# Spacing the splits of cross-attention weights evenly over a feed-forward block, and resharing the taps of a convolution

## The reference, cut to what matters

```
# first block, its end
h2 = rmsnorm(x, g_ffn)
ff = silu(h2 @ w_ffn_gate) * (h2 @ w_ffn_up)        # 1024 -> 2816
x  = x + ff @ w_ffn_down                            # 2816 -> 1024
# second block, layer 0
h = rmsnorm(x, norm_mix_g)
u = h @ w_pw1 + b_pw1;  a, gate = split(u);  u = a * sigmoid(gate)
u = conv_general_dilated(u, w_dw, width 31, causal, one filter a channel) + b_dw
u = silu(layernorm(u));  x = x + u @ w_pw2 + b_pw2
...
# keys and values of a memory of 256 rows, in both layers (nothing here depends on x)
k = rmsnorm(mem, g_l) @ w_k_l;   v = rmsnorm(mem, g_l) @ w_v_l
```

## Time and profile before

| what | value |
|---|---|
| median, range of three runs | 2281.22 us, 2280.41 to 2285.22 |
| the profiled execution, whole | 2279.9 us |
| its span from first to last instruction | 2277.7 us |
| TensorE busy | 2219.8 us (97%) |
| VectorE, ScalarE, GpSimd busy | 1340.5, 975.5, 406.4 us |
| mean granted TensorE clock | 0.996 |

### The profile page before, as it was taken

How to read it: one execution, slowest core, us unless ns; L and a number is a source line. 1 busy time by engine, 2 the same in 40 slices (tenths; PEclk the granted TensorE clock), 3 DMA queues, 4 the chain that set the end, 5 groups by cost and what they waited for, 6 DMA issues and landing times.

```text
span 2277.7 us, 31273 instructions
## 1 busy us (share of the span) xinstructions
PE 2219.8 (97%) x10680; PEld 1800.2 (79%) x10680; DVE 1340.5 (59%) x1904; ACT 975.5 (43%) x1486; POOL 406.4 (18%) x338
## 2 busy tenths in 40 slices
PE   8999999998998999989999999999999999999998
PEld 6787788877776878868888888887777888888887
DVE  5567756554555679975465445485655646454455
ACT  6775654432333367763332222245454333222222
POOL 2232102101010247834040000040000304000003
PEclk9999999999999999999999999999999999999999
DMA  4222223467676455642123333332222212333332
GB/s 148 65 66 63 76 80 96 145 177 230 179 204 200 148 173 187 215 156 74 56 82 95 93 101 102 92 87 77 66 56 60 88 57 83 102 93 98 96 96 89
DMA packets 413080, 253.36 MB, mean 111 GB/s; under 512 B 14832, under 2 KB 394224, under 8 KB 412976
## 3 DMA queue, kind: packets, MB, share of 16 engines
q1 hardware_dynamic: 412080, 249.68, 36.7%
q0 software_dynamic: 896, 2.33, 0.3%
HBM read 232.56 MB, written 18.87 MB: 110 GB/s over the span
## 4 chain that ended last, share of the span: by engine, by line
PE 78%; DMA 7%; DVE 5%; issue 3%; ACT 2%; SPq 1%; POOLq 1%; DVEq 1%; POOL 0%; ACTq 0%
PE bank L1951 22%; PE bank L1953 21%; PE bank L1952 21%; DMA m_raw<-in_w_ffn_up 3%; PE bank L1931 2%; DVE m_w_lo L1260 2%; DMA m_raw<-in_w_ffn_down 2%; PE bank L2424 1%; POOLq L670 1%; PE bank L2401 1%; DMA mem_low<-m_mem_raw_lo 1%; PE bank L2339 1%; PE bank L2329 1%; PE bank L2104 1%; PE bank L2530 1%
## 5 line engine op out<-in xcount | busy, mean ns | idle before, releaser
L695 ACT ACTIVATE m_w_hi<-m_raw 128x1024 fp32r<-128x1024 f32 x332 | 351.4, 1059 | 844.1 <-PE bank L1953 693.8
L1951 PE MATMUL bank<-m_h_hi,m_w_hi 128*128 128x512 f32 x1504 | 608.2, 404 | 17.1 <-DVE m_w_lo L1260 15.8
L1953 PE MATMUL bank<-m_h_hi,m_w_lo 128*128 128x512 f32 x1504 | 587.0, 390 | 0.0
L1952 PE MATMUL bank<-m_h_lo,m_w_hi 128*128 128x512 f32 x1504 | 586.4, 390 | 0.0
L1260 DVE TENSOR_TENSOR m_w_lo<-m_raw,m_w_hi 128x1024 fp32r<-128x1024 f32 x332 | 444.7, 1339 | 133.3 <-ACT m_w_hi L695 127.4
L1951 PEld LDWEIGHTS bank<-m_h_hi,m_w_hi 128*128 128x128 f32 x1504 | 282.6, 188 | 94.0 <-DVE m_w_lo L1260 19.9
L1953 PEld LDWEIGHTS bank<-m_h_hi,m_w_lo 128*128 128x128 f32 x1504 | 282.3, 188 | 60.1
L1952 PEld LDWEIGHTS bank<-m_h_lo,m_w_hi 128*128 128x128 f32 x1504 | 282.9, 188 | 54.8 <-issue 2.2
L1951 PE MATMUL bank<-m_f_hi,m_w_hi 128*128 128x512 f32 x688 | 269.5, 392 | 7.4 <-DVE m_w_lo L1260 7.3
L1953 PE MATMUL bank<-m_f_hi,m_w_lo 128*128 128x512 f32 x688 | 267.9, 389 | 0.0
L1952 PE MATMUL bank<-m_f_lo,m_w_hi 128*128 128x512 f32 x688 | 267.8, 389 | 0.0
(11 more groups left out here) (399 smaller groups left out, 3222.6 us busy)
## 6 DMA issues: line engine op xcount, KB each, us to landing
m_raw<-in_ff_w SPq DMA_DIRECT2D x256, 256.0 KB, 3.0
mem_low<-m_mem_raw_lo SPq DMA_DIRECT2D x32, 512.0 KB, 3.3
m_mem_w_low<-mem_low SPq DMA_DIRECT2D x32, 512.0 KB, 7.3
m_raw<-in_conv_pw_w SPq DMA_DIRECT2D x48, 256.0 KB, 3.1
m_raw<-in_w_in SPq DMA_DIRECT2D x47, 256.0 KB, 3.3
m_raw<-in_w_ffn_gate SPq DMA_DIRECT2D x44, 256.0 KB, 5.2
m_raw<-in_w_ffn_up SPq DMA_DIRECT2D x44, 256.0 KB, 5.1
m_raw<-in_w_ffn_down SPq DMA_DIRECT2D x40, 256.0 KB, 5.1
```

The costliest lines, as they stand in the source:

```text
L695: act.activation(WH[:, v % 2], RAW[:, v % 2], ACT.Copy).then_inc(s.w_hi, 1)
L1951: pe.matmul(o, high[:, r, k, :], hi, start=start, stop=False)
L1952: pe.matmul(o, high[:, r, k, :], lo, start=False, stop=False)
L1953: last = pe.matmul(o, low[:, r, k, :], hi, start=False, stop=stop)
```

## The change

`MEM_SPLIT_AT` names every second unit from 4 to 66. Before, it named 4 to 14 in steps of 2, every unit from 16 to 23, 24 to 38 in steps of 2, every unit from 40 to 47, and 48 and 50. The stores stand one place later on SyncE's list. So the last splits and stores reach into the loads of the convolution stage, and `conv_loads` passes them out.

In the convolution, each of the first seven tiles gives 12 taps to ScalarE and GpSimd (13 before) and 19 to VectorE (18 before). The last tile gives 8 to ScalarE and GpSimd (10 before), 6 to TensorE (3 before) and 17 to VectorE (18 before). On ScalarE the high part of memory piece 0 stands ahead of the norm's root, that of piece 25 ahead of the last tile's sigmoid, and the last tile's first four products ahead of piece 26.

```diff
-SUM_TAPS = 13
-SUM_TAPS_LAST = 10
+SUM_TAPS = 12
+SUM_TAPS_LAST = 8
-MEM_SPLIT_AT = (4, 6, 8, 10, 12, 14) + tuple(range(16, 24)) + tuple(range(24, 40, 2)) + tuple(range(40, 48)) + (48, 50)
+MEM_SPLIT_AT = range(4, 4 + 2 * MEM_UNITS, 2)
-PE_TAPS_LAST = 3
+PE_TAPS_LAST = 6
@@ SyncE
-                split_at.setdefault(ffn + n + 5, []).append(lambda i=i: split_out(i))
+                split_at.setdefault(ffn + n + 6, []).append(lambda i=i: split_out(i))
@@ mem_load
+                stored(i)
@@ last group
-                    assert not split_at
-                    for i in range(MEM_UNITS - 4, MEM_UNITS):
-                        stored(i)
@@ conv_loads
                 for half in range(2):
+                    splits()
@@ after conv_loads(0), conv_loads(1)
+            while split_at:
+                for f in split_at.pop(min(split_at)):
+                    f()
+            for i in range(MEM_UNITS - 4, MEM_UNITS):
+                stored(i)
@@ VectorE conv_steps
-                cut = [0, 9, DVE_TAPS]
+                cut = [0, 10, DVE_TAPS]
@@ ScalarE conv_steps
                 if m == 0:
+                    mem_high(first)
                     norm()
...
-                mem_high(first)
+                if m > 0:
+                    mem_high(first)
...
+                if m == KD - 1:
+                    mem_high(last)
                 act.wait_ge(s.cv_g, m + 1)
...
             last = SUM_TAPS_LAST, PE_TAPS_LAST
-            mem_high(25)
+            products(KD - 1, 0, 4, *last)
             mem_high(26)
-            products(KD - 1, 0, 4, *last)
             mem_out(24)
-            products(KD - 1, 4, 7, *last)
+            products(KD - 1, 4, 6, *last)
             mem_high(27)
-            products(KD - 1, 7, SUM_TAPS_LAST, *last)
+            products(KD - 1, 6, SUM_TAPS_LAST, *last)
```

## The result

The kernel after takes 2249.03 us (median of four runs, 2247.36 to 2250.44), the kernel before in the same series 2283.03 us (four runs, 2280.41 to 2285.22). The ratio is 0.9851, with a 95% interval of 0.9834 to 0.9868: faster by 34 us. The forecast was 2254 us with a gain of 27.6.

What follows compares the result with a forecast made beforehand. TensorE, busy 2219.8 of 2277.7 us, was taken as the bound. The terms -24.5 + 3.5 - 2.8 + 0.8 - 4.6 = -27.6 us took 2279.9 to 2252.3, given as 2254 on the median's side; range 2246 to 2267.

Steps and rivals of the forecast that it cites:

- The feed-forward's waits: Feed-forward stretches with splits: stores behind the up load remove all 22.5 us of waits, plus restarts, -24.5 us.
- Rival C: Feed-forward: the spacing does nothing, 32 splits still cost 24 us, only tail and start pay, 2278 us; chance 0.04.
- D: Feed-forward: the up unit's load lands too late at each of 32 splits, slower, 2297 us; chance 0.03.
- the term for restarts: Feed-forward: each restart after a wait costs TensorE 0.11 us, times 22 is 2.4 us.
- The 0.4 us kept for a stray wait: Feed-forward: of 24.9 us of waits and restarts, 0.4 us was held back for a stray wait.
- The added splits: 722 to 803 us, last group: eight more splits cost +3.5 us, 1.5 at unit 60's load and 2.0 on VectorE.
- Rival B: Last eight units: VectorE becomes the bound by its exclusion with GpSimd, +6 instead of +2, 2263 us; chance 0.07.
- The convolution's start: TensorE starts 1.2 us sooner with piece 0's high part early, 1.6 us of clock return, -2.8 us (0 to -4).
- The middle: Convolution tiles: VectorE bounds tiles 2 to 4, one tap more costs 2.0 us, less 1.2 us elsewhere, +0.8 us.
- tiles 2 to 4 no shorter than before: Sign expected in the profile after: convolution tiles 2 to 4 don't get shorter; no size given.
- The tail: Last tile to squares' sum: products run while a landing is awaited, two sums fewer, -4.6 us (-2 to -7).
- rival A: Feed-forward: half of the waits remain, -12 in place of -24.5, 2266 us; chance 0.08.

Runs made afterwards that it cites:

- Experiment 1: The kernel after with each store back at its old place, ahead of the up load, even spacing kept: 2276.54 us.
- experiment 2: The kernel after with the old table of splits, stores behind the up load except in the rows of eight: 2253.44 us.
- experiment 10: The kernel of experiment 3 with VectorE's first seven low parts of the normed memory set between the down units: 2244.6 us.
- experiment 3: The kernel after with all 32 splits done before the last group's down units: 2242.38 us.
- experiment 6: The kernel after with 13 products a tile on ScalarE, 12 additions on GpSimd and one VectorE tap fewer, last tile as changed: 2250.67 us.
- experiment 7: The kernel after with the last tile's old division (10 products on ScalarE, 3 taps on TensorE, 18 on VectorE), new order kept: 2247.82 us.
- experiments 4: The kernel of experiment 3 with the six DMAs for memory pieces 0 to 2 spread over the last group's down units: 2240.66 us.
- experiment 9: The kernel after with the high parts of memory pieces 29 to 31 moved later on ScalarE, among and behind the squares: 2246.23 us.

## Why the prediction was right, and where it was not

**The feed-forward's waits: 24.5 us forecast, 29.1 found (331.28 to 302.14).** The mechanism is the one forecast. In after the up load is issued at 559.73, the store at 560.87 behind it; ScalarE's high part then waits for TensorE, no longer for a landing as in the earlier trace rows.

```profile
559.73 0.92 SPq L399 DMA_DIRECT2D m_raw<-in_w_ffn_up  x2
560.87 0.34 SPq L489 DMA_DIRECT2D mem_low<-m_mem_raw_lo  x1
```

```profile
566.58 1.06 ACT L699 ACTIVATE m_w_hi<-m_raw 128x1024 fp32r<-128x1024 f32 x1 [2.91 <-PE bank L1960]
```

Experiment 1 shows that most of it is the store's place (22.4 us), and experiment 2 that the evenly spaced waits vanish with it. Rival C describes the kernel of experiment 1, not this one; D is out. The size was off by 4.6 us, nearly all of it in the term for restarts, which I set to 0.11 us a wait. TensorE in after, at the boundary of two units:

```profile
571.53 0.39 PE L1960 MATMUL bank<-m_h_hi,m_w_lo 128*128 128x512 f32 x1
571.76 0.39 PE L1958 MATMUL bank<-m_h_hi,m_w_hi 128*128 128x512 f32 x1
```

Without a wait the next matmul starts 0.16 us before the end of the one before it. The profile counts idle time from that end, so a wait costs the idle time, the 0.16 us of lost overlap, the 0.11 us by which the second matmul comes later, and 0.03 us spread over the next four. That is 0.30 us for each of 22 waits, 6.7 us instead of 2.4: 22.5 + 6.7 = 29.1. The 0.4 us kept for a stray wait was not needed, since none came. The 6.7 us are counted as busy time. The clock at the convolution's start takes 1.4 of them back, the last group's new waits 0.9 and the stretch ahead of unit 4 0.4; in the tail three more taps (2.6 us) and the full clock that came back there nearly cancel (0.2). Together with hundredths elsewhere that leaves the 3.8 us above.

**The added splits: +3.5 forecast, +4.2 found.** From unit 59 to the first down unit's start after loses 1.71 us (1.5 forecast). Across the kernels with the same program up to there this wait was 1.04 to 1.98 us. SyncE is held up issuing behind the store, ScalarE waits, TensorE waits:

```profile
729.38 0.71 SPq L489 DMA_DIRECT2D mem_low<-m_mem_raw_lo  x1
730.13 4.04 SPq L399 DMA_DIRECT2D m_raw<-in_w_ffn_down  x2
```

```profile
740.37 1.06 ACT L699 ACTIVATE m_w_hi<-m_raw 128x1024 fp32r<-128x1024 f32 x1 [7.97 <-DMA m_raw<-in_w_ffn_down]
```

```profile
742.74 0.50 PE L1958 MATMUL bank<-m_f_hi,m_w_hi 128*128 128x512 f32 x1 [1.70 <-DVE m_w_lo L1267]
```

The rest, 2.5 us, is VectorE (2.0 forecast). A low part of a memory piece takes 2.31 us there:

```profile
764.12 2.31 DVE L1603 TENSOR_TENSOR m_mem_raw_lo<-m_mem_raw,m_mem_raw_hi 128x1024 fp32r<-128x1024 f32 x1
```

```profile
763.79 1.55 POOL L595 TENSOR_TENSOR m_sumsq<-m_sumsq,m_sq 128x512 f32<-128x512 f32 x1
```

GpSimd's sum started first and ends at 765.34; 1.22 us from there is 766.56, and the row ends at 766.43. The Trainium skill's "SBUF — State Buffer", section "SBUF: two separate sides", says that whichever of the two starts first keeps the other out for its whole length; it says so of a VectorE instruction with two SBUF inputs and a GpSimd one that reads SBUF. Here and in experiment 10 (0.4 us of work, 1.5 us long) the trace agrees to 0.2 us. TensorE lost 0.87 and 0.79 us, two restarts and some tenths to it; the rule's upper end of 6 us was not reached. Rival B's direction was thus real and its price too high; experiment 3 shows that the whole term was avoidable.

**The convolution's start: -2.8 forecast, +0.8 found. This step failed.** The forecast put TensorE's start at VectorE's lows plus one split of 1.2 to 1.5 us. The mechanism held: high part early, VectorE late.

```profile
782.78 2.30 DVE L1603 TENSOR_TENSOR m_mem_raw_lo<-m_mem_raw,m_mem_raw_hi 128x1024 fp32r<-128x1024 f32 x1
...
785.04 3.21 DVE L1609 SCALAR_TENSOR_TENSOR m_mn_lo<-m_mem_cols,m_vec,m_mn_hi 128x256 fp32r<-128x256 f32 x8
```

But the last split took 2.30 us beside GpSimd, so the wait only fell from 3.79 to 3.13 us. Net, the arrival is 0.55 us sooner instead of 1.2. And the clock, from which I took 1.6 us back, did not come back; it cost 1.4 us more. The ten microseconds behind the first memory product in the kernel before:

```profile
813.50:823.50 10.00, 10.00 (x49) 9.04 (x50) 1.22 (x1) 3.08 (x4) 0.00 (x0) 0.84 0.49 159
```

The same ten microseconds behind the same matmul in after:

```profile
788.30:798.30 10.00, 9.99 (x43) 9.12 (x44) 1.79 (x2) 2.81 (x4) 0.00 (x0) 0.69 0.48 145
```

and in experiment 6, then in experiment 7, both with the same 3.13 us wait:

```profile
787.40:797.40 10.00, 9.96 (x48) 8.90 (x49) 1.82 (x2) 2.83 (x4) 0.00 (x0) 0.83 0.52 158
```

```profile
787.00:797.00 10.00, 10.00 (x55) 8.79 (x56) 2.66 (x4) 4.07 (x6) 0.00 (x0) 1.00 0.49 159
```

One wait, three outcomes: 27.9, 26.6 and 25.1 us for the stage, with the same instructions up to there in all three. I treated the granted clock as a result of the wait's length and so as something an edit could return; at 3.1 us something decides that these runs don't show. The clock did stay at its full level in the kernels that waited 1.3 to 1.9 us there (experiments 2 to 4, all 25.11 us); experiment 1 waited 2.49 us there and lost it (26.64 us).

**The middle: +0.8 forecast, -1.4 found.** The step that failed is that VectorE bounds tiles 2 to 4. It was read from its busy share. What ends TensorE's waits there is ScalarE's high part, and ScalarE is late by its products and by waiting for GpSimd's additions (12.8 us before, 1.2 after). One product and one addition fewer a tile are worth 2.1 us in the middle and 1.3 in the tail (experiment 6); the forecast gave the shorter chain 1.2 us and took 2.0 off for VectorE. It had named a shorter GpSimd chain only as its lower bound. With thirteen products the middle takes 0.7 us more than in the kernel before, so something else in the change costs about that; the runs don't say what, and it is within the range of this stage. The sign "tiles 2 to 4 no shorter than before" did not come true: the three tiles from the third on take 62.95 us and took 63.52.

**The tail: -4.6 forecast, -4.8 found** (46.10 to 41.34). One wait of 1.95 us ended by ScalarE, none for the last tile, as forecast:

```profile
972.21 1.12 PE L2391 MATMUL bank<-m_ln_sq,m_con 128*128 128x512 f32 x2 [1.95 <-ACT m_ln_sq L1100]
```

```profile
950.66 2.57 ACT L1038 ACTIVATE m_tap_product<-m_padded,m_vec 128x512 f32<-128x512 f32 x4 [1.09 <-DVE m_padded L1684]
...
968.69 2.95 ACT L1014 ACTIVATE m_mem_w_high<-m_mem_w 128x1024 fp32r<-128x1024 f32 x3 [1.61 <-DMA m_mem_w_low<-mem_low]
971.55 0.61 ACT L1100 ACTIVATE m_ln_sq<-m_conv 128x512 f32<-128x512 f32 x1
```

The four products run at 950.66, ahead of the landings; the three high parts and then the first square are the floor that the forecast named as last, and experiment 9 took it away. Within the term the way was not as told: TensorE idles 4.9 us less, of which 2.5 us is ScalarE's copy of the key piece's product, awaited 3.08 us before and 0.58 us after, which the forecast did not list. The three taps cost 2.6 us, and 2.4 us came back from the clock, which was at its slow level (1.2 GHz) behind the 4.39 us wait ahead of the mean and is at full speed in after (1.00). That the total was met to 0.2 us is partly luck.

**The sum.** From unit 4 on: -29.1 + 4.2 + 0.8 - 1.4 - 4.8 = -30.2 us, from unrounded terms; a difference of 0.3 us ahead of it and 0.1 behind make it the 29.8 of the two spans. The errors are -4.6 (feed-forward, restarts above all), +0.7 (added splits), +3.6 (start), -2.2 (middle) and -0.2 (tail). They leave -2.6 us of a sum of absolute errors of over 11: that the total came so near is luck in the start and the middle. The remaining 4 us to the medians' 34 lie in how the kernel before ran in the first series: its profiled execution was 3.1 us under its median of 2283.0, and after's was 0.7 us above its own.

**The forecast's own arithmetic.** Its range of 2248 to 2261 leaves out the -12 that it names as the first term's bound (that is rival A). With the other bounds in squares the upper end comes out as 2261, the lower as 2249.6, and the measured 2249.03 lies just below that, inside the 2246 to 2267 that was given. The 0.88 us a split at which D "decides slower" is where D meets the kernel before; for 4.6 us more it takes 1.02.

## What to carry to other kernels

A load that starts late can be the fault of what stands ahead of it in its own queue: put what waits for a late result (here a store) behind what can already go, before changing how often it occurs. Price a wait of TensorE as its idle time plus what the restart loses (0.30 us here), and don't count on getting a slow clock back when an edit shortens the wait by only some tenths. Ask not which engine is busiest but which one ends the wait, and what on its list stands ahead of the awaited step without being needed yet.

## What was not expected of the hardware

A wait of 3.13 us at the same place of the same program was followed by a granted clock over 10 us of 1.00, 0.83 or 0.69, from one kernel to the next; 3.08 us in the tail of the kernel before was followed by full speed (0.36 us for the first matmul of 128x256, where a slow one takes 0.55), 3.49 us in experiment 7 by the slow clock. Waits of 1.34 to 1.93 us at the first product were followed by 1.00, but the slow level (1.2 GHz) also followed 2.49 us in experiment 1 (26.64 us for the stage) and 1.96 us ahead of the squares' sum in experiment 2: the granted clock over the ten microseconds behind it was 0.83. The 1.95 and 1.96 us at the same place in after and in experiments 4 and 6 kept the full clock.

A VectorE instruction with two SBUF inputs of 0.4 us took 1.5 us when it met one of GpSimd's in progress, so seven spread out among GpSimd's squares took 1.1 us more of VectorE's time each than in a row behind them.
